# Memory's squares on ScalarE, moved behind its roundings and the second weight rounding

## What is computed

```python
def rmsnorm(x, g):
    x32 = x.astype(jnp.float32)
    y = x32 * lax.rsqrt(jnp.mean(x32 * x32, axis=-1, keepdims=True) + NORM_EPS)
    return (y * g.astype(jnp.float32)).astype(x.dtype)

def cross_attention(xn, memn, w_q, w_kv, w_o):   # memn = rmsnorm(mem, norm_mem)
    k, v = jnp.split(memn @ w_kv, 2, axis=-1)
    ...
```

## Time and profile before

| | |
|---|---|
| median of 3 runs | 2147.3 us (2144.9 to 2148.8) |
| the profiled execution | 2145.07 us, span 2143.2 us |
| TensorE busy | 2103.9 us |
| VectorE, ScalarE, GpSimd busy | 1248.0, 869.7, 114.1 us |
| TensorE's mean granted clock | 0.993 |

### The profile page before, as it was taken

One profiled execution on the slowest core, in us unless ns is written; L12 is line 12 of the kernel. 1 busy time (PEld: TensorE's weight loads), 2 busy tenths in 40 slices (PEclk: granted clock), 3 DMA queues, 4 the chain that ended last, 5 costly groups with the idle time before them and its releaser, 6 DMA issues. The chain is left out here.

```text
span 2143.2 us, 27369 instructions
## 1 busy us (share of the span) xinstructions
PE 2103.9 (98%) x10160; PEld 1713.2 (80%) x10160; DVE 1248.0 (58%) x2010; ACT 869.7 (41%) x1341; POOL 114.1 (5%) x117
## 2 busy tenths in 40 slices
PE   8999999999999999999999999999999999999998
PEld 7988888877777778878888887777777878888886
DVE  7886776766666445453333347778666564343444
ACT  7432222253344442342222236665775444232233
POOL 2000000022000000010000002000002010000001
PEclk9999999999999999999999999999999999999999
DMA  8655444534222223323333323122223213333332
GB/s 342 216 184 180 162 166 160 184 103 119 89 71 78 89 90 126 99 69 99 98 98 98 98 82 106 60 60 79 80 69 118 69 59 91 105 93 95 98 98 69
DMA packets 66777, 238.41 MB, mean 111 GB/s; under 512 B 7848, under 2 KB 10024, under 8 KB 65904
## 3 DMA queue, kind: packets, MB, share of 16 engines
q1 hardware_dynamic: 60768, 218.81, 31.9%
q0 software_dynamic: 3728, 16.08, 2.4%
q10 hardware_dynamic: 2176, 2.10, 0.3%
HBM read 230.12 MB, written 4.21 MB: 109 GB/s over the span
## 5 line engine op out<-in xcount | busy, mean ns | idle before, releaser
L1275 DVE TENSOR_TENSOR wlo<-raw,whi 128x1024 fp32r<-128x1024 f32 (+1 forms) x352 | 428.9, 1218 | 262.6 <-ACT whi L629 259.7
L2175 PE MATMUL bank<-hhi,whi 128*128 128x512 f32 (+1 forms) x1408 | 544.3, 387 | 5.5 <-DVE hlo L1284 4.2
L629 ACT ACTIVATE whi<-raw 128x1024 fp32r<-128x1024 f32 (+1 forms) x352 | 367.2, 1043 | 433.5 <-PE bank L2177 383.2
L2177 PE MATMUL bank<-hhi,wlo 128*128 128x512 f32 (+1 forms) x1408 | 538.5, 382 | 0.0
L2176 PE MATMUL bank<-hlo,whi 128*128 128x512 f32 (+1 forms) x1408 | 538.3, 382 | 0.0
L2175 PE MATMUL bank<-ghi,whi 128*128 128x512 f32 x1016 | 399.6, 393 | 2.9 <-DVE wlo L1275 2.9
L2177 PE MATMUL bank<-ghi,wlo 128*128 128x512 f32 x1016 | 396.1, 390 | 0.0
L2176 PE MATMUL bank<-glo,whi 128*128 128x512 f32 x1016 | 396.0, 390 | 0.0
L2175 PEld LDWEIGHTS bank<-hhi,whi 128*128 128x128 f32 x1408 | 266.6, 189 | 58.1 <-DVE wlo L1275 6.8
L2177 PEld LDWEIGHTS bank<-hhi,wlo 128*128 128x128 f32 x1408 | 266.9, 190 | 51.3
L2176 PEld LDWEIGHTS bank<-hlo,whi 128*128 128x128 f32 x1408 | 266.9, 190 | 49.6 <-issue 0.2
(11 more groups left out here) (331 smaller groups left out, 2031.0 us busy)
## 6 DMA issues: line engine op xcount, KB each, us to landing
raw<-w SPq DMA_DIRECT2D x389, 512.0 KB, 3.6
work<-w SPq DMA_DIRECT2D x12, 512.0 KB, 11.4
raw<-w SPq DMA_DIRECT2D x16, 384.0 KB, 3.1
gated_in<-gated_in POOLq DMA_DIRECT2D x40, 64.0 KB, 1.9
gated_in<-w SPq DMA_DIRECT2D x4, 512.0 KB, 9.8
xT<-x_t POOLq DMA_DIRECT2D x1, 2048.0 KB, 12.0
kv_hbm<-work POOLq DMA_DIRECT2D x2, 1024.0 KB, 4.8
work<-w POOLq DMA_DIRECT2D x4, 512.0 KB, 5.0
```

What stands on the lines that cost most here:

```text
L629: nc.scalar.activation(whi[v % 2][:, 0:kc * P], raw[u % 4][:, 0:kc * P], ACT.Copy).then_inc(w_hi, 1)
L1275: nc.vector.tensor_tensor(wlo[v % 2][:, 0:kc * P], raw[u % 4][:, 0:kc * P], whi[v % 2][:, 0:kc * P].bitcast(F32), ALU.subtract).then_inc(w ...
L2175: nc.tensor.matmul(dst, wh[:, ws], hi[:, c, :], start=c == 0, stop=False)
L2177: ins = nc.tensor.matmul(dst, wl[:, ws], hi[:, c, :], start=False, stop=c == kc - 1)
```

## The change

On ScalarE, at the very start of the kernel, rounding and square of a piece of memory no longer alternate. All eight roundings come first, then the rounding of the second key weight, then the eight squares. Only the order on this engine is changed; the other engines' programs are as they were.

```diff
             act.wait_ge(mods_done, 1)
             for c in range(DC):
                 scaled_hi(N_MEM, c)
+            split(V_XK + 1)
+            for c in range(DC):
                 norm_square(N_MEM, c)
-            split(V_XK + 1)
```

## The result

The changed kernel takes 2148.3 us (median of 22 runs, 2144.0 to 2151.3) against 2144.8 for the kernel before in the same comparisons (22 runs, 2141.6 to 2149.2): a ratio of 1.0016, 95% interval 1.0011 to 1.0022, so 3.5 us or 0.16% slower. That is within the 0.2% named as no change that shows, on the side that was forecast; the forecast loss was 2.5 us.

The account below looks back on a forecast made before the run. TensorE, busy 98% of the span, was taken as the bound. Its 1.3 us at memory's sum lay within 2.5 us from the late x: 2147.3 + 2.5 = 2149.8 us, range 2145.8 to 2153.5.

Parts of the forecast that it names:

- Roundings, first unit: Start: ScalarE's roundings in 0.49 us steps, low halves done at about 15.8, TensorE's first unit over at 18.2, gaining 1.0 us.
- Adds: GpSimd's six adds of squares take turns with VectorE's long instructions, the last ending at 24.5 instead of 18.45 us.
- Memory's sum: TensorE waits from 22.3 to 24.6 us for the sixth add; its third unit starts 1.3 us late.
- rival (c): TensorE's new wait keeps its clock low over the following 36 matmuls, 3.4 us more; 2152.0 us, chance 0.12.
- The load of x: GpSimd issues x at 24.4 instead of 18.39 us, landing at 35; TensorE's fifth unit starts 2.5 us late.
- Rival (b): x lands by 33.8 us, so only the wait at memory's sum remains, +1.3 us; 2148.6 us, chance 0.13.
- Sum: Whole kernel: TensorE 2.5 us late at 43 us, kept to the end; 2149.8 us, chance 0.47.
- Catch up by 60 us: ScalarE's later weight roundings are late by the same 3 us, with similar slacks, and recover by 60 us.

Follow-up runs that it names:

- the wait filled: Changed kernel plus 27 extra 256-column matmuls into an unused PSUM bank just ahead of memory's sum on TensorE; ratio to the kernel before 1.0008 (0.9998 to 1.0017).
- the sum later: Changed kernel with memory's sum of squares on TensorE taken behind the whole second unit and modulation tiles 2 and 3; ratio to the kernel before 1.0012 (1.0003 to 1.0021).
- x held back: Kernel before the change, with only GpSimd's load of x held until memory's sum is done on TensorE; ratio to the kernel before 1.0007 (0.9998 to 1.0017).

## Why the prediction was right, point by point

Direction, range and the start of the chain (roundings, adds, the wait at the sum) came out as forecast. That the size came out near, 2.5 against 3.5 us, is partly luck: the wait that was to set it, of the fifth unit for the late x, did not occur, and slow matmuls that the sum did not count took its place.

- *Roundings, first unit.* Right. Steps of 0.49 us, low halves done at 15.7, the unit over at 17.9 instead of the forecast 18.2.
- *Adds.* Right, in mechanism and size: last end forecast 24.5, measured 24.4. The adds take 7.64 us beside VectorE's long instructions and 5.08 beside none, and 5.52 with all but the weight subtraction held back. The page "SBUF — State Buffer" of the Trainium skill, section "SBUF: two separate sides", has an exclusive lock: whichever of the two instructions starts first holds the shared ports to its end. The trace agrees: adds of 1.52 us that end 0.59 and 0.58 us behind a product. The step rested on one add of the trace before that met a long VectorE instruction, and that was enough.
- *Memory's sum.* Mechanism right, size off: wait of 3.25 us, forecast 2.3. I gave the tile's products and the half unit the 4.05 us of before; at full clock they took 3.2 (17.93 to 21.1), so TensorE was there 1.2 us earlier. That changes nothing in the end of the wait (24.55 against 24.6), nor in what the wait costs against the kernel before: 1.25 us, forecast 1.3.
- *Clock.* Held as rival (c) at 0.12, and partly true: 16 of the third unit's 24 matmuls ran slowly. This is the term missing from the sum: TensorE's own lateness was forecast as 1.3 us at the third unit and the fifth, and measured as 2.0 and 3.55, of which 2.30 are slow matmuls. (c) priced them at 3.4 us, if the whole third unit were slow, and held that less would disappear in the wait for the fifth unit. It was less and did not disappear; it made that wait disappear. The run with the wait filled shows the cause: TensorE is ready 2.65 us earlier, of which x leaves 1.34.
- *The load of x.* Issue right to 0.05 us, landing at 34.1 instead of 35 (9.7 us after the issue, between the bounds 8.7 and 12.0). The forecast wait before the fifth unit did not come: the subtraction was ready at 42.0 (forecast 43.0, x having landed 0.9 us sooner) and TensorE only came at 44.17. Rival (b) had no such wait either, but its condition, a landing by 33.8 us, did not hold: the wait is missing because TensorE was 3.55 us late and not 1.3. By itself the chain through x would have cost 1.4 us here (2.07 late, less its slack of 0.69); where it does decide, with the wait filled and with the sum later, it makes the fifth unit 2.4 and 2.6 us later than before. The page "DMA: Bandwidth & Descriptors" of the Trainium skill, section "Anatomy of one DMA — SWDGE (gpsimd) path", gives a fixed 2.0 us plus the bytes by 436 GB/s, an estimate of 6.8 us; the trace does not agree (9.7 us, and 8.5 to 12.2 over all runs).
- *Sum.* 2.5 forecast, 3.5 in the medians, 3.55 in the profile. The forecast chain (x) gave a loss near the true one by a delay that lay hidden behind the other; with the other gone it decides.
- *"Catch up by 60 us".* Wrong for the weight roundings, of which it was said: they are 3.5 us late from 49 us on, and still are at 80, since they follow TensorE's units. TensorE's own lateness is still there at 410 us, as the first paragraph of the prediction had it.

## What to carry to other kernels

Moving a step on one engine moves everything that its results start: here six adds went from beside VectorE's short instructions to beside its long ones, and a load that stood behind them went 6 us with them. Before such a move, list what runs on the engine that takes turns with the one that does the follow-up work. When a bound engine gets a new wait, price the matmuls behind it at the lower clock too, and when one delay is removed look for the next that it covered. For effects of 0.2%, compare marks at the end of the changed stretch and medians; one execution's total can differ by as much where the clock dips at another place.

## What the runs showed of the hardware that was not expected

- The granted clock reads 1.00 at the start of every profile, also where the matmuls are 0.21 us apart: with x held back it reads 1.00 from 19 to 25 us while tile 1's products took 3.41 us instead of 1.84. That no change of level had been recorded up to there is a guess that fits; no run shows why. At the start of this kernel the step between matmuls tells the clock, not that column.
- The level of the clock differs from one execution to the next at the same place in the program: 0.66 and 1.00 in the window at 460 us in the two profiles of the kernel before, with spans of 2143.2 and 2141.4 us.
